# Two of the four score joins of a chunked recurrence moved from VectorE's predicated copies to plain ScalarE copies

## The chip, the core and the metric

The kernel runs on one core of one Trainium2 chip. Its metric is the device time of one launch in microseconds. Engines are named as in the profile: TensorE (PE, with PEld for its weight loads), VectorE (DVE), ScalarE (ACT), GpSimd (POOL), SyncE (SP).

## What is computed

The program is a model of two blocks, the first of two layers and the second of one. The change concerns one half of the first layer's mixer, a gated linear recurrence over 768 tokens (256 of context, 512 of the sequence) in 4 heads of 128 columns, once forwards and once backwards. Cut to what matters:

```python
def gla_chunked(q, k, v, log_f, s0):
    def step(state, inp):
        qc, kc, vc, gc = inp
        b = jnp.cumsum(gc, axis=2)
        diff = b[:, :, :, None, :] - b[:, :, None, :, :]
        decay = jnp.where(prefix_mask, jnp.exp(jnp.minimum(diff, 0.0)), 0.0)
        scores = jnp.einsum('bhtk,bhsk,bhtsk->bhts', qc, kc, decay)
        out = (jnp.einsum('bhtk,bhkv->bhtv', qc * jnp.exp(b), state)
               + jnp.einsum('bhts,bhsv->bhtv', scores, vc))
        b_last = b[:, :, -1:, :]
        new_state = (jnp.exp(b_last[:, :, 0, :])[..., None] * state
                     + jnp.einsum('bhsk,bhsv->bhkv', kc * jnp.exp(b_last - b), vc))
        return new_state, out
```

The scores have a decay that depends on the query, the key and the column, so they are no single matrix product. The kernel splits the lower triangle of a chunk into blocks, each with a reference token of its own, for which the decay falls into a factor of the query and a factor of the key.

## The kernel before, in words

**The stretch.** `recurrence_and_mix` interleaves four programs on each engine: `flow` (L456 matmuls: 8 tiles of a projection with 1024 x 128 weights split in a high and a low part, three matmuls each), `flow_g` (4 more such tiles), `gl`, an object of the class `Recurrence`, and `cm` (`ChunkMix`, a small token mixer, its matmuls L1511 to L1536). Each program yields at slots; `even` gives each slot a due time, `merged` sorts all slots by due time, and `weave` writes the instructions of each engine in that order. So each engine has one order written out by hand, and an instruction that waits holds up all that stand behind it on its engine, whichever program they belong to. The due times of `gl` are 8 us a slot before the first step and 14.3 us after.

**The recurrence.** Chunks are of 128 tokens; there are 6 of them and two directions, so 12 steps n = 0 to 11, directions alternating. A slot has eight turns, and `turns` gives for each engine what it does in which turn and how many steps ahead. In slot s, for step n = s unless said:

- VectorE: turn 0 `merge` (L1278 four times, L1281), turn 1 `decayed_base` of the next step (L1245, L1246), turn 2 `decayed` of the next step (L1256 eight times, L1258, L1259; the products of queries and keys with their decays), turn 3 `keys` three steps ahead (L1198), turn 4 `both` and `update` (L1289; L1299, the state, four instructions), turns 5 to 7 the log sums of later steps (L1228, L1233, L1217, L1218, L1207).
- ScalarE: turn 0 `grow_base` of the next step (L1319 to L1321), turn 1 `grow` of the next step (L1327 and L1328, the exponentials, the last 128 x 2560), turn 4 `take` (L1339) and `log` (L1311), turn 6 `keys_back` of the next step (L1333, which copies the turned keys from PSUM).
- TensorE: turn 2 `read_out` (L1358, L1359), turn 3 `gain` (L1366), turn 5 `turn_keys` (L1375, four transposes; it waits for the update L1299) and the scores of joins 0 and 1 of the next step (L1386), turn 6 the scores of joins 2 and 3 (L1386), turn 7 the base scores (L1406).

Between these, ScalarE evicts the projections' accumulators with Gelu (L1451) or Silu (L1584), which need another table (ACT_TABLE_LOAD; L52 loads the table of Ln and Exp back), and makes w_hi, the high part of a coming weight tile (L337). GpSimd makes w_lo from it (L378).

**The joins.** `JOINED` is (128, 64, 32, 16), the sizes of the blocks that are joined from halves; inside blocks of `BASE` = 8 tokens the base scores stand. For each join the scores lie in half a PSUM bank (`ps_s[0]` holds joins 0 and 1, `ps_s[1]` joins 2 and 3; 64 late queries for each of the 4 heads, so 256 columns), for all 128 keys on the partitions. Only those of keys in the early half of the same block are wanted. `merge` writes them into S (an SBUF tile of 128 x 512) with a predicated copy under a mask, four in turn, each waiting for the one before it (the counter `merged`), and then the base scores (L1281). `read_out` multiplies S with the values. `scored` counts the three groups of scores of a step.

Of the kernel before, what the change touches and what calls it, by code (L numbers as in the profile page):

```python
# [7 lines left out]
ACT = mybir.ActivationFunctionType  # L8
# [8 lines left out]
CHUNK = 128  # L17
# [750 lines left out]
A_HEADS = 4  # L768
# [334 lines left out]
class Recurrence:  # L1103
# [3 lines left out]

    def __init__(self, K, c, q, v, z, masks, masks_in, work, taken):  # L1110
        nc = self.nc = K.nc
        self.K, self.q, self.v, self.z, self.masks_in = K, q, v, z, masks_in
        H = A_HEADS
        self.NL = NL = len(JOINED)
        self.W = W = H * CHUNK
        self.steps, self.first = TOK // CHUNK, CTX // CHUNK
        self.n = 2 * self.steps
        LATE = CHUNK // 2
        self.masks = masks
        U32 = mybir.dt.uint32  # L1120
        self.mask = [[masks[:, d, l * LATE:(l + 1) * LATE].bitcast(U32) for l in range(NL)]
                     + [masks[:, d, NL * LATE:NL * LATE + CHUNK].bitcast(U32)] for d in range(2)]
        self.rel = [taken(f"rel{d}", NL + 3, work) for d in range(2)]
        self.k, self.S, self.state = ([taken(f"{n}{d}", 1, work)[:, 0, :] for d in range(2)]
                                      for n in ("k", "S", "state"))
        self.kt = taken("kt", 1, work)[:, 0, :]
        self.eb_end = [c.enter_context(nc.sbuf_tensor(f"gl_eb_end{d}", [P, H], F32)) for d in range(2)]
        bank = [c.enter_context(nc.psum_tensor(f"gl_bank{m}", [P, 512], F32)) for m in range(4)]
        self.ps_s, self.ps_u, self.ps_o = bank[0:2], bank[2], bank[3]
        (self.loaded, self.zeroed, self.k_done, self.logged, self.summed, self.related, self.grown, self.ends,  # L1130
         self.mixed, self.scored, self.merged, self.k_turned, self.kt_done, self.o_done, self.o_taken, self.u_done,
         self.updated) = K.signals("gl", "loaded zeroed k_done logged summed related grown ends mixed scored merged "
                                   "k_turned kt_done o_done o_taken u_done updated")

    SLOTS = range(-3, 12)

# [49 lines left out]
    def dve(self, dve):  # L1186
# [74 lines left out]
        def merge(n):  # L1261
            d = n % 2
            S = self.S[d]
            LATE = CHUNK // 2
            if n >= 2:
                dve.wait_ge(self.o_done, n - 1)
            for l, size in enumerate(JOINED):
                if l % 2 == 0:
                    dve.wait_ge(self.scored, 3 * n + l // 2 + 1)
                if l:  # L1270
                    dve.wait_ge(self.merged, 5 * n + l)
                nb, h = CHUNK // size, size // 2
                late, _ = self.late(d, size)
                out = self.heads(S).rearrange("p h (n e) -> p h n e", e=size)[:, :, :, late]
                mask = self.mask[d][l].rearrange("p (n e) -> p n e", e=h).unsqueeze(1).to_broadcast([P, H, nb, h])
                at = (l % 2) * H * LATE
                got = self.ps_s[l // 2][:, at:at + H * LATE].rearrange("p (h n e) -> p h n e", h=H, e=h)
                nc.vector.copy_predicated(out, mask, got).then_inc(self.merged, 1)  # L1278
            dve.wait_ge(self.scored, 3 * n + 3)
            dve.wait_ge(self.merged, 5 * n + NL)  # L1280
            nc.vector.copy_predicated(self.heads(S), self.mask[d][NL].unsqueeze(1).to_broadcast([P, H, CHUNK]),  # L1281
                                      self.heads(self.ps_o[:, :])).then_inc(self.merged, 1)

# [22 lines left out]
    def act(self, act):  # L1306
        nc, NL = self.nc, self.NL

        def log(n):
            act.wait_ge(self.k_done, n + 1)  # L1310
            nc.scalar.activation(self.of_z(n), self.of_z(n), ACT.Ln).then_inc(self.logged, 1)  # L1311

        def grow_base(n):
            d = n % 2
            act.wait_ge(self.related, 2 * n + 1)
            if n >= 2:
                act.wait_ge(self.updated, n - 1)
            end = 0 if d else CHUNK - 1
            nc.scalar.activation(self.eb_end[d][:, :], self.of_z(n)[:, :, end], ACT.Exp)  # L1319
            nc.scalar.activation(self.rel[d][:, NL + 1, :], self.rel[d][:, NL, :], ACT.Exp, scale=-1.0)  # L1320
            nc.scalar.activation(self.rel[d][:, NL + 2, :], self.rel[d][:, NL + 2, :], ACT.Exp).then_inc(self.grown, 1)  # L1321

        def grow(n):
            d = n % 2
            act.wait_ge(self.related, 2 * n + 2)
            act.wait_ge(self.grown, 2 * n + 1)
            nc.scalar.activation(self.of_z(n), self.of_z(n), ACT.Exp)  # L1327
            nc.scalar.activation(self.rel[d][:, 0:NL + 1, :], self.rel[d][:, 0:NL + 1, :],  # L1328
                                 ACT.Exp).then_inc(self.grown, 1)

        def keys_back(n):
            act.wait_ge(self.k_turned, n + 1)
            nc.scalar.activation(self.kt, self.ps_u[:, :], ACT.Copy).then_inc(self.kt_done, 1)  # L1333

        def take(n):
            if self.earlier(n) is not None:
                return
            act.wait_ge(self.o_done, n + 1)
            nc.scalar.activation(self.of_z(n), self.heads(self.ps_o[:, :]), ACT.Copy).then_inc(self.o_taken, 1)  # L1339
        yield from self.turns({0: [(1, grow_base)], 1: [(1, grow)], 4: [(0, take), (3, log)],  # L1340
                               6: [(1, keys_back)]})

    def pe(self, pe):
        nc, H, NL = self.nc, A_HEADS, self.NL
# [4 lines left out]

        def read_out(n):  # L1350
            d = n % 2
            pe.wait_ge(self.merged, 5 * n + 5)
            pe.wait_ge(self.mixed, n + 1)
            if n >= 2:
                pe.wait_ge(self.updated, n - 1)
            for h in range(H):
                c = self.col(h)
                nc.tensor.matmul(self.ps_o[:, c], self.state[d][:, c], self.of_z(n)[:, h, :], start=True, stop=False)  # L1358
                last = nc.tensor.matmul(self.ps_o[:, c], value(n, h), self.S[d][:, c], start=False, stop=True)  # L1359
            last.then_inc(self.o_done, 1)  # L1360
# [29 lines left out]
        def scores(n, half):  # L1390
            if n == 0 and half == 0:
                self.K.keep_busy(self.ps_s[0][:, 0:P], 18)
            pe.wait_ge(self.mixed, n + 1)
            if n:
                pe.wait_ge(self.merged, 5 * (n - 1) + 2 * half + 2)
            for l in (2 * half, 2 * half + 1):
                last = score(n, l)
            last.then_inc(self.scored, 1)
# [2539 lines left out]
```

## Time and profile before

| | us |
|---|---|
| median of 3 runs | 2659.57 |
| lowest and highest run | 2657.66 and 2663.55 |
| profiled execution, its own time | 2655.66 |
| profiled execution, its span | 2653.9 |

In the rows further down, a line of the timeline gives start and duration in us, engine, line, operation, output<-input, and in brackets the idle time of the engine before it with what ended it. A line of the waits says who waited for whom: us in total, times, longest. A line of the groups has count, busy us, mean ns of one, then the idle time before them. A line of the stages gives the stretch, its length, busy us of each engine with its count, the granted clock of TensorE (1.00 is full) and DMA. Matmuls are pipelined, so the duration of a group of them is longer than their number times their spacing.

### The profile page before, as it was taken

To read this page: it belongs to the slowest core of one execution; us is meant where nothing else is said; L and a number is where in the kernel's file an instruction comes from. 1 tells how busy PE (TensorE), PEld (TensorE's weight loads), DVE (VectorE), ACT (ScalarE), POOL (GpSimd) and SP (SyncE) were. 2 spreads that over 40 slices of the span, in tenths; PEclk is the share of its full clock that TensorE was granted. 3 is DMA by queue.
4 is the path that set the end of the run, shared out by engine and by line. 5 is a ranking of instruction groups with operands and counts; after the bars stand their busy time and mean duration, and the time that the engine had idled before them with its cause. 6 is when DMAs were issued, how large, how long until landed. Compare 5 with 4: busy or idle time off the path is not lost. (4 is left out here: it accounts for less than half of the span.)

```text
span 2653.9 us, 36467 instructions
## 1 busy us (share of the span) xinstructions
PE 2516.1 (95%) x14777; PEld 2127.7 (80%) x14777; DVE 1677.8 (63%) x2692; ACT 989.1 (37%) x1362; POOL 183.3 (7%) x185
## 2 busy tenths in 40 slices
PE   8999897999999999989999999999989988989997
PEld 3888786888888888866679989977778886867786
DVE  5887797467667776534446756737977775354744
ACT  4235555332212222345434323325532224345532
POOL 0111013000000000012000000001510000000000
PEclk9999999999999999999999999999999999999999
DMA  7650012223353333221023443322210001212232
GB/s 266 197 156 24 18 33 70 90 88 92 103 154 112 104 105 102 75 71 48 1 72 125 134 148 126 114 85 72 87 59 17 9 17 40 95 60 68 80 104 79
DMA packets 62682, 232.26 MB, mean 88 GB/s; under 512 B 6962, under 2 KB 9650, under 8 KB 61875
## 3 DMA queue, kind: packets, MB, share of 16 engines
q1 hardware_dynamic: 47538, 175.40, 20.2%
q0 software_dynamic: 14976, 54.53, 6.5%
q8 instruction: 117, 1.92, 0.3%
q14 instruction: 51, 0.41, 0.1%
HBM read 227.02 MB, written 2.10 MB: 86 GB/s over the span
## 5 line engine op out<-in xcount | busy, mean ns | idle before, releaser
L393 DVE TENSOR_TENSOR w_lo<-w_raw,w_hi 128x1024 fp32r<-128x1024 f32 (+2 forms) x253 | 323.0, 1277 | 322.2 <-ACT w_hi L337 318.1
L337 ACT ACTIVATE w_hi<-w_raw 128x1024 fp32r<-128x1024 f32 (+4 forms) x284 | 298.1, 1050 | 254.6 <-PE late_acc L474 93.4
L474 PE MATMUL mid_acc<-mid_h_hi,w_hi 128*128 128x258 f32 x832 | 279.7, 336 | 1.5 <-DVE mid_od_fq L642 1.0
L474 PE MATMUL mid_acc<-mid_h_hi,w_lo 128*128 128x258 f32 x832 | 279.3, 336 | 0.0
L474 PE MATMUL mid_acc<-mid_h_lo,w_hi 128*128 128x258 f32 x832 | 277.4, 333 | 0.0
L474 PE MATMUL late_acc<-late_h_hi,w_hi 128*128 128x258 f32 x704 | 199.4, 283 | 0.0
L474 PE MATMUL late_acc<-late_h_hi,w_lo 128*128 128x258 f32 x704 | 198.7, 282 | 0.0
L474 PE MATMUL late_acc<-late_h_lo,w_hi 128*128 128x258 f32 x704 | 197.9, 281 | 0.0
L474 PEld LDWEIGHTS mid_acc<-mid_h_hi,w_hi 128*128 128x128 f32 x832 | 157.5, 189 | 19.3 <-issue 2.4
L474 PEld LDWEIGHTS mid_acc<-mid_h_lo,w_hi 128*128 128x128 f32 x832 | 157.7, 190 | 18.5 <-issue 1.2
L474 PEld LDWEIGHTS mid_acc<-mid_h_hi,w_lo 128*128 128x128 f32 x832 | 157.0, 189 | 16.0
L474 PEld LDWEIGHTS late_acc<-late_h_lo,w_hi 128*128 128x128 f32 x704 | 133.8, 190 | 0.5 <-issue 0.5
L474 PEld LDWEIGHTS late_acc<-late_h_hi,w_hi 128*128 128x128 f32 x704 | 133.3, 189 | 0.5 <-issue 0.5
L474 PEld LDWEIGHTS late_acc<-late_h_hi,w_lo 128*128 128x128 f32 x704 | 132.9, 189 | 0.0
L474 PE MATMUL mid_acc<-mid_y_hi,w_lo 128*128 128x256 f32 (+1 forms) x384 | 128.8, 336 | 0.0
L474 PE MATMUL mid_acc<-mid_y_hi,w_hi 128*128 128x256 f32 (+1 forms) x384 | 128.0, 333 | 0.7 <-PEq L1744 0.7
L474 PE MATMUL mid_acc<-mid_y_lo,w_hi 128*128 128x256 f32 (+1 forms) x384 | 128.6, 335 | 0.0
L131 DVE CUSTOM_DVE_ANT_0 mid_scratch<-mid_side_raw,mid_rows 128x1024 f32<-128x1024 f32 x96 | 117.4, 1223 | 1.9 <-DVE mod L136 0.3
L2991 ACT ACTIVATE dr_low<-dr_bank 128x512 f32<-128x512 f32 x48 | 28.7, 597 | 173.0 <-PE dr_bank L3122 173.0
L474 PE MATMUL dq_acc<-s_h_hi,w_hi 128*128 128x512 f32 x200 | 85.8, 429 | 5.6 <-DVE s_h_lo L2577 4.2
L474 PE MATMUL qvz_acc<-ev_h_hi,w_hi 128*128 128x256 f32 (+1 forms) x256 | 87.2, 341 | 0.0
L474 PE MATMUL qvz_acc<-ev_h_lo,w_hi 128*128 128x256 f32 (+1 forms) x256 | 86.9, 340 | 0.0
(531 smaller groups left out, 6187.4 us busy)
## 6 DMA issues: line engine op xcount, KB each, us to landing
w_raw<-in_up SPq DMA_DIRECT2D x88, 512.0 KB, 3.6
mid_side_raw<-in_ada_t POOLq DMA_DIRECT2D x48, 512.0 KB, 3.9
w_raw<-in_down SPq DMA_DIRECT2D x32, 704.0 KB, 4.1
qvz_side_raw<-in_ada_t POOLq DMA_DIRECT2D x32, 512.0 KB, 4.0
w_raw<-in_dn_qkv SPq DMA_DIRECT2D x25, 512.0 KB, 3.2
late_side_raw<-in_ada_t POOLq DMA_DIRECT2D x24, 512.0 KB, 3.9
w_raw<-in_da SPq DMA_DIRECT2D x18, 512.0 KB, 3.3
w_raw<-in_ev_qvz SPq DMA_DIRECT2D x16, 512.0 KB, 4.2
```

The costliest lines, as they stand in the source:

```text
L131: nc.vector.tensor_tensor_reduce(out=self.scratch, in0=self.raw[:, j, :], in1=self.rows[:, m, :], scale=1.0, scalar=0.0, op0=ALU.mult, op1 ...
L337: nc.scalar.activation(K.whi[:, g % 2, 0:width], K.raw[:, g % 2, 0:width], ACT.Copy).then_inc(K.hi_done, 1)
L393: nc.vector.tensor_tensor(K.wlo[:, g % 2, 0:width], K.raw[:, g % 2, 0:width], K.whi[:, g % 2, 0:width].bitcast(F32), ALU.subtract).then_in ...
L474: last = nc.tensor.matmul(self.acc[i % len(self.acc)][:, at:at + width], left[:, j, cols], right[k][:, moving:moving + width], start=(k == ...
L2991: nc.scalar.activation(XL[G][:, :], bank[G][0][:, :], ACT.Copy).then_inc(A[G].empty, 1)
```

## The change

Joins 0 and 1 (sizes 128 and 64) have halves of 64 and 32 keys, which are whole ranges of partitions. For them ScalarE now writes the wanted scores to S with plain copies: one of 64 partitions x 256 (join 0) and two of 32 partitions x 128 (join 1), in the new `place`, in turn 6 of the slot before, behind `keys_back` of the same step. `place` waits for `scored` of joins 0 and 1 and, from step 2 on, for the read-out of the step that used the same S. It signals `placed`. On VectorE `merge` waits for `placed` and for the scores of joins 2 and 3, and does joins 2 and 3 and the base: three predicated copies instead of five. On TensorE the scores of joins 0 and 1 wait for `placed` of the step before, those of joins 2 and 3 and the read-out for the new counts of `merged`.

```diff
+    PLACED = 2
+    MERGES = len(JOINED) - PLACED + 1
...
@@ merge, on VectorE
-            if n >= 2:
-                dve.wait_ge(self.o_done, n - 1)
-            for l, size in enumerate(JOINED):
-                if l % 2 == 0:
-                    dve.wait_ge(self.scored, 3 * n + l // 2 + 1)
-                if l:
-                    dve.wait_ge(self.merged, 5 * n + l)
+            dve.wait_ge(self.placed, n + 1)
+            dve.wait_ge(self.scored, 3 * n + 2)
+            for l in range(self.PLACED, NL):
+                size = JOINED[l]
+                if l > self.PLACED:
+                    dve.wait_ge(self.merged, self.MERGES * n + l - self.PLACED)
...
-            dve.wait_ge(self.merged, 5 * n + NL)
+            dve.wait_ge(self.merged, self.MERGES * n + NL - self.PLACED)
...
@@ on ScalarE
+        def place(n):
+            d = n % 2
+            if n == 0:
+                act.wait_ge(self.zeroed, 1)
+            if n >= 2:
+                act.wait_ge(self.o_done, n - 1)
+            act.wait_ge(self.scored, 3 * n + 1)
+            for l in range(self.PLACED):
+                size = JOINED[l]
+                nb, h = CHUNK // size, size // 2
+                late, early = self.late(d, size)
+                out = self.heads(self.S[d]).rearrange("p h (n e) -> p h n e", e=size)
+                at = l * A_HEADS * (CHUNK // 2)
+                got = self.ps_s[0][:, at:at + A_HEADS * (CHUNK // 2)].rearrange("p (h n e) -> p h n e", h=A_HEADS, e=h)
+                for m in range(nb):
+                    keys = slice(m * size + early.start, m * size + early.stop)
+                    last = nc.scalar.activation(out[keys, :, m, late], got[keys, :, m, :], ACT.Copy)
+            last.then_inc(self.placed, 1)
...
-                               6: [(1, keys_back)]})
+                               6: [(1, keys_back), (1, place)]})
...
@@ on TensorE
-            pe.wait_ge(self.merged, 5 * n + 5)
+            pe.wait_ge(self.merged, self.MERGES * (n + 1))
...
-                pe.wait_ge(self.merged, 5 * (n - 1) + 2 * half + 2)
+                if half == 0:
+                    pe.wait_ge(self.placed, n)
+                else:
+                    pe.wait_ge(self.merged, self.MERGES * (n - 1) + NL - self.PLACED)
```

## Rows read from the trace of the kernel before

**Rows 1.** The page, busy us, share of the span and instructions of each engine:

```profile
PE 2516.1 (95%) x14777; PEld 2127.7 (80%) x14777; DVE 1677.8 (63%) x2692; ACT 989.1 (37%) x1362; POOL 183.3 (7%) x185
```

**Rows 2.** The stages (stretch; busy us of PE, PEld, DVE, ACT, POOL; clock; DMA):

```profile
205.00:437.50 232.50, 219.73 (x1535) 198.45 (x1533) 177.50 (x412) 125.99 (x169) 27.27 (x12) 0.98 0.08 24
```

**Rows 3.** The waits from 205 to 445 us:

```profile
ACT x L1333 <- PE gl_bank L1375: 21.9, 7, 7.2
...
DVE x L1281 <- PE gl_bank L1406: 8.5, 8, 2.1
...
DVE ev_rest L1256 <- ACT ev_rest L1328: 7.3, 7, 2.7
...
PE gl_bank L1375 <- DVE ev_rest L1299: 4.3, 4, 2.3
```

**Rows 4.** The timeline of step n = 6 on TensorE, ScalarE and VectorE:

```profile
341.35 0.60 PE L1375 MATMUL gl_bank<-ident,ev_rest 128*128 128x128 f32 x4
341.79 1.90 PE L1386 MATMUL gl_bank<-ev_rest 128*128 128x64 f32 x16
...
341.99 0.60 ACT L1333 ACTIVATE x<-gl_bank 128x512 f32<-128x512 f32 x1 [1.60 <-PE gl_bank L1375]
342.61 1.28 ACT L1451 ACT_TABLE_LOAD   x1
343.90 0.88 ACT L1451 ACTIVATE x<-uv_acc 128x512 f32<-128x512 f32 x2
...
348.92 2.33 ACT L1328 ACTIVATE ev_rest<-ev_rest 128x2560 f32<-128x2560 f32 x1
...
351.28 0.43 DVE L1256 TENSOR_TENSOR ev_rest<-ev_q,ev_rest 128x256 f32<-128x256 f32 x1
...
356.11 1.12 DVE L1299 SCALAR_TENSOR_TENSOR ev_rest<-ev_rest,gl_eb_end,gl_bank 128x128 f32<-128x128 f32 x4 [0.39 <-PE gl_bank L1366]
...
357.29 0.66 PE L1375 MATMUL gl_bank<-ident,ev_rest 128*128 128x128 f32 x4 [0.50 <-DVE ev_rest L1299]
```

**Rows 5.** The groups by line and shape, 205 to 445 us:

```profile
L1278 DVE COPY_PREDICATED x<-rstd,gl_bank 128x256 f32<-128x256 uint32 x48 | 21.2, 441 | 18.8 <-PE gl_bank L1386 17.2
...
L1451 ACT ACTIVATE x<-uv_acc 128x512 f32<-128x512 f32 x7 | 4.2, 597 | 0.1
...
L1451 ACT ACTIVATE x<-uv_acc 128x256 f32<-128x256 f32 x7 | 2.7, 379 | 0.0
```

**Rows 6.** The timeline of VectorE, joins of n = 6, base copy of n = 7:

```profile
347.17 1.97 DVE L1278 COPY_PREDICATED x<-rstd,gl_bank 128x256 f32<-128x256 uint32 x4
...
367.36 0.75 DVE L1281 COPY_PREDICATED x<-rstd,gl_bank 128x512 f32<-128x512 uint32 x1 [1.02 <-PE gl_bank L1406]
```

**Rows 7.** The timeline of the three engines, single rows of other steps:

```profile
268.22 0.58 ACT L1481 ACTIVATE x<-cm_ps,eps 128x384 f32<-128x384 f32 x1 [5.03 <-PE cm_ps L1511]
...
325.32 0.66 PE L1375 MATMUL gl_bank<-ident,ev_rest 128*128 128x128 f32 x4 [2.32 <-DVE ev_rest L1299]
...
360.54 1.06 ACT L337 ACTIVATE w_hi<-w_raw 128x1024 fp32r<-128x1024 f32 x1 [1.96 <-PE uv_acc L456]
...
386.82 0.43 DVE L1256 TENSOR_TENSOR ev_rest<-ev_q,ev_rest 128x256 f32<-128x256 f32 x1 [0.48 <-ACT ev_rest L1328]
...
400.36 2.33 ACT L1328 ACTIVATE ev_rest<-ev_rest 128x2560 f32<-128x2560 f32 x1
...
403.51 0.41 DVE L1256 TENSOR_TENSOR ev_rest<-ev_q,ev_rest 128x256 f32<-128x256 f32 x1
...
414.85 0.38 ACT L1584 ACTIVATE x<-uv_acc 128x256 f32<-128x256 f32 x1 [1.35 <-PE uv_acc L456]
```

**Rows 8.** A stall in TensorE's timeline, and the stages after two stalls:

```profile
363.93 0.47 PE L456 MATMUL uv_acc<-ev_h_hi,w_hi 128*128 128x512 f32 x1 [1.75 <-ACT x L1451]
...
365.50:368.50 3.00, 3.00 (x13) 2.71 (x12) 1.95 (x4) 2.91 (x4) 0.00 (x0) 0.50 0.42 164
...
325.50:329.00 3.50, 3.50 (x27) 3.24 (x27) 3.50 (x10) 2.95 (x5) 0.00 (x0) 1.00 0.00 0
```

More of the change, by code:

```diff
@@ L1131, in __init__ @@
          self.mixed, self.scored, self.merged, self.k_turned, self.kt_done, self.o_done, self.o_taken, self.u_done,
-         self.updated) = K.signals("gl", "loaded zeroed k_done logged summed related grown ends mixed scored merged "
-                                   "k_turned kt_done o_done o_taken u_done updated")
+         self.updated, self.placed) = K.signals("gl", "loaded zeroed k_done logged summed related grown ends mixed scored merged "
+                                   "k_turned kt_done o_done o_taken u_done updated placed")
     SLOTS = range(-3, 12)
```

## The prediction

> **What bounds the kernel now.** The page first: TensorE is busy for 95% of the span [rows 1]. The first layer's recurrence is only the stretch from 205 to 437.5 us; there the stages row shows TensorE busy for 219.7 of 232.5 us, VectorE for 177.5 and ScalarE for 126.0 [rows 2]. So in this stretch time is lost or won only where TensorE stands still, and next I read which wait ends last there. In the waits of the stretch TensorE waits for VectorE's state update (L1299) before it turns the keys (L1375), for 4.3 us in all; VectorE in its turn waits for ScalarE's large exponential (L1328) before the scaling products (L1256), 7.3 us in 7 waits; and ScalarE waits for TensorE's turned keys (L1375) before it copies them (L1333), 21.9 us [rows 3]. These three waits close a ring: turned keys, copy, other ScalarE work, exponentials, products, update, next turned keys.
>
> The timeline of one step (n = 6) shows the ring go round [rows 4]. TensorE turns the keys at 341.35 and then does the scores of the first two joins, 341.79 to 343.69. ScalarE copies the keys at 341.99 and goes straight on to a table load at 342.61, the two Gelu evictions, w_hi, and the exponentials, whose last ends at 351.25. VectorE starts the products at 351.28, the moment the last exponential is there, is through them and a later step's keys at 355.72, waits 0.39 us for TensorE and updates from 356.11 to 357.23. TensorE, which has stood for 0.50 us, turns the next keys at 357.29. Everything in this ring from 342.61 to 351.25 is ScalarE in program order, with no wait in it.
>
> **What goes.** Two predicated copies of 128x256 on VectorE per step: 24 of them at 441 ns [rows 5], 10.6 us of VectorE; with their wait for each other they stand 0.49 us apart (four take 1.97 us [rows 6]), so 0.98 us per step. Is any of it on the path? No. What follows the joins is the base copy (L1281), and that needs the base scores, which TensorE does last: at n = 7 the base copy waits 1.02 us for them [rows 6], and 8.5 us in 8 waits over the stretch [rows 3]. At n = 6 the four joins end at 349.14 and the copy follows in line, but behind it come only L1245 and L1246 before VectorE needs L1328, which ends at 351.25 [rows 4]. So the freed 0.98 us ends in waits that are there already: I credit 0. The bound on the gain: five steps (n = 4, 5, 6, 8, 9) have four joins in one run, 4.9 us if VectorE set the pace in all of them.
>
> **What is added.** Three plain copies from PSUM per step on ScalarE: 64 partitions x 256, and 32 x 128 twice, 36 in all. The trace has no such copy. ScalarE's time goes by elements of a partition: 597 ns for 512, 379 for 256 [rows 5], so 0.85 ns each and by extension 270 ns for 128. An ACTIVATE behind another starts about 0.10 us before that ends (597 + 379 = 976 ns, but the two evictions take 0.88 us together [rows 4]). So three in a row take 0.28 + 0.17 + 0.27 = 0.72 us, say 0.71. Bounds: 0.55 us if narrow copies are cheaper, 0.92 us if nothing overlaps. The page "ScalarE: Activation LUTs" of the Trainium skill, section "Rules for kernel authors", tells authors to leave such simple work to VectorE and prices each ACTIVATE at about 0.3 us plus 0.83 ns an element; by that three would take about 1.33 us, and the sum below would be some 3 us larger. The 597 ns row lies below what that gives for 512 elements (0.72 us), so I keep to the rows.
>
> **The added wait** is the larger part. The copies stand right behind the keys' copy and wait for the scores of the first two joins. At n = 6 these end at 343.69, the keys' copy at 342.59: ScalarE stands 1.14 us (with 0.04 us for the signal, as between the end of L1375 at 341.95 and 341.99), copies for 0.71 us, and starts the table load at 344.46 instead of 342.61: **1.85 us late**. Queued behind it on ScalarE are the evictions, w_hi (GpSimd's w_lo and the next weight load wait for that; these have a tile of 16 us to spare) and the exponentials, for which VectorE waits, for which TensorE waits. No DMA is moved.
>
> Step by step, what reaches TensorE's next turn of the keys:
> - n = 0 to 3: another activation holds the keys' copy up until the scores are done, and 0.7 us goes into ScalarE's next waits, such as 5.03 us before 268.22 [rows 7]. At n = 0 alone such a wait comes only after the exponentials. 0.
> - n = 4: scores long done, the copies advance ScalarE by 0.60 us (what follows overlaps the last), and the products waited on L1328 as at n = 8; TensorE's 2.32 us stall at 325.32 grows: 0.6 [rows 7].
> - n = 5 and 6: 1.85 less VectorE's 0.39 us of slack before the update; n = 5 runs as n = 6 does, with 0.05 us more between update and turn: 1.4 and 1.5 [rows 4].
> - n = 7: ScalarE waits 1.96 us for TensorE before w_hi at 360.54 anyway, and the copies fit before it: 0 [rows 7].
> - n = 8: the products at 386.82 wait on L1328 and VectorE has no slack after them: 1.85 [rows 7].
> - n = 9: L1328 would end at 404.54 instead of 402.69; VectorE began the products at 403.51, when itself ready: 1.05 [rows 7].
> - n = 10: the wait of 1.35 us before the second eviction at 414.85 absorbs most: 0.4 [rows 7].
> - n = 11: the same wait, longer: 0.
>
> Sum: 0.6 + 1.4 + 1.5 + 1.85 + 1.05 + 0.4 = **6.8 us** longer. TensorE is already in its order of work, so nothing fills these stalls.
>
> **The clock.** After TensorE's 1.75 us stall before 363.93, a step with a 0.50 us stall before it, the granted clock falls to the lower level (1.2 GHz); it is 0.50 from 365.5 to 368.5 [rows 8]. After the stall of 2.32 us before 325.32 it stays full [rows 8]. Three microseconds at half clock lose 1.5 us of matmuls. The change makes five stalls of 1 us or more at L1375: 2.32 + 0.6 = 2.9 after n = 4, then 1.4, 0.5 + 1.5 = 2.0, and 1.85 and over 1.05 after n = 8 and 9. One of these two brought a fall; part of the loss lies beside ScalarE's chain. I take two falls worth 1 us each, between 0 and 5 x 1.5 = 7.5: +2.
>
> The sum is made against the profiled execution, 2655.66 us with a span of 2653.9; that gives 2664.5. The median of the runs is 3.9 us higher at 2659.57, and the same 8.8 us on it gives 2668.4: **2668.0 us**.
>
> **Rivals.**
> 1. VectorE sets the pace (faster). If ScalarE's delay were taken up by slack, each step with joins in one run would save 0.98 us; TensorE's waits for the update (4.3 us) cap it there: 2659.6 - 4.3 = 2655.3. For it: VectorE is the engine that TensorE waits for at L1375 [rows 3], and all five steps have their joins in one run. Against it: the products start on L1328's end at n = 6 and 8 [rows 4, 7], and VectorE waits for it 7 times in all [rows 3]. It decides if ScalarE's chain is under 0.1 us late at the products. Chance 0.07.
> 2. Nothing to be measured. The delay is half absorbed: only n = 5, 6 and 8 carry it, less VectorE's 0.98 where it helps, and no fall of the clock, (1.4 + 1.5 + 1.85) less 0.98 = 3.8 us: 2663.4. A measurement of this kernel can tell about 0.2%, 5.3 us, from no change, and my sum without the clock is only 1.5 us above that. Chance 0.2.
> 3. The ring with more clock falls: each new stall brings one, inside the scores for which ScalarE now waits, so that the loss goes into the ring in full: 6.8 + 7.5 = 14.3 us, 2673.9. Chance 0.15, part of slower.
> 4. The forecast, 0.58.
>
> **Numbers.** Slower 0.73 (forecast and rival 3), same 0.20, faster 0.07. The range 2661 to 2675 holds most of rival 2 at its lower end and rival 3 at its upper; it leaves out rival 1 and combinations with dearer copies.
>
> **What would show it.** In the profile after: three ACTIVATEs beside L1333 per step, the first waiting for L1386 about 1.1 us at n = 5, 6, 8, 9, 10; L1278 with 24 instead of 48; L1256's wait for L1328 up from 7.3 to about 15 us; TensorE's wait for L1299 at L1375 up from 4.3 to 10 or more; the stretch 205 to 437.5 longer by 7 to 9 us, nothing changed before 315 us. It is wrong if the step from one L1375 to the next stays at 16.0 us around n = 5 and 6, or if L1256 no longer waits for ScalarE.

## The result, and the profile after

The changed kernel takes 2675.19 us (median of 4 runs, 2674.52 to 2678.01) against 2658.61 us before: a ratio of 1.0057 with an interval of 1.0044 to 1.0069. It is **slower**: by 0.57%, 15 us, by the ratio, and by 16.6 us between the medians. Run once more, beside other runs of the kernel before, it gave 1.0063 (1.0048 to 1.0078). The line numbers of the kernel after have moved: the turned keys are L1396, the joins' scores L1407, the keys' copy L1335, the large exponential L1330, the products L1259, the update L1301, joins 2 and 3 L1280, the new copies L1353.

The profiled execution took 2675.26 us with a span of 2673.5. From the first turning of the keys to the last update it is 240.28 us long, against 226.31 before. The page's first part, and the stages of these two stretches, after and then before:

```profile
PE 2535.0 (95%) x14777; PEld 2141.2 (80%) x14777; DVE 1667.4 (62%) x2668; ACT 999.5 (37%) x1398; POOL 183.3 (7%) x185
```

```profile
211.58:451.86 240.28, 225.63 (x1510) 204.11 (x1508) 161.12 (x371) 135.10 (x203) 26.13 (x11) 0.94 0.06 21
```

```profile
210.10:436.41 226.31, 214.63 (x1510) 193.92 (x1508) 171.53 (x396) 124.89 (x167) 26.38 (x11) 0.98 0.07 22
```

So 14.0 us of the difference lie in the stretch. VectorE has 10.4 us less to do there, as foreseen, and ScalarE 10.2 us more, against 8.5 by the forecast's 0.71 us a step. TensorE, with the same number of matmuls, is busy 11.0 us longer, and its granted clock is 0.94 instead of 0.98: its work has not grown, it runs slower. Its idle time has grown by 3.0 us. (The rest of the difference between these two executions, 5.6 us, lies outside, 1.5 us ahead of the stretch and 4.2 us behind it, where the programs are the same; runs of the kernel before spread from 2656.5 to 2668.2 us.)

The waits of the kernel after, 205 to 465 us (the rows that answer to [rows 3], with the new ones):

```profile
ACT x L1335 <- PE gl_bank L1396: 20.7, 7, 7.3
...
DVE x L1283 <- PE gl_bank L1430: 16.2, 10, 3.8
...
ACT x L1353 <- PE gl_bank L1407: 11.8, 7, 2.8
DVE ev_rest L1259 <- ACT ev_rest L1330: 10.3, 9, 3.4
...
PE gl_bank L1396 <- DVE ev_rest L1301: 8.6, 5, 2.8
```

The third line is the wait that the change adds, 11.8 us of ScalarE. (VectorE's joins now wait for the copies too, 12.6 us in 3 times, all at steps 0 to 4.) TensorE's wait for the update has doubled, from 4.3 to 8.6 us. And VectorE's base copy (L1283), which waited 8.5 us for the base scores, now waits 16.2: that is where VectorE's freed time went, for the most part.

Step n = 6 in the timelines of ScalarE, VectorE and TensorE, to be laid beside [rows 4]:

```profile
345.68 0.66 PE L1396 MATMUL gl_bank<-ident,ev_rest 128*128 128x128 f32 x4 [0.29 <-DVE ev_rest L1301]
346.18 1.90 PE L1407 MATMUL gl_bank<-ev_rest 128*128 128x64 f32 x16
...
346.38 0.60 ACT L1335 ACTIVATE x<-gl_bank 128x512 f32<-128x512 f32 x1 [1.11 <-PE gl_bank L1396]
348.17 0.81 ACT L1353 ACTIVATE x<-gl_bank 64x256 f32<-64x256 f32 x3 [1.20 <-PE gl_bank L1407]
349.00 1.28 ACT L1475 ACT_TABLE_LOAD   x1
...
355.31 2.33 ACT L1330 ACTIVATE ev_rest<-ev_rest 128x2560 f32<-128x2560 f32 x1
...
357.67 0.42 DVE L1259 TENSOR_TENSOR ev_rest<-ev_q,ev_rest 128x256 f32<-128x256 f32 x1 [0.49 <-ACT ev_rest L1330]
...
363.20 0.81 PE L1396 MATMUL gl_bank<-ident,ev_rest 128*128 128x128 f32 x4 [2.07 <-DVE ev_rest L1301]
```

ScalarE stands 1.20 us for the scores, copies for 0.81 us, and loads the table at 349.00, 3.32 us after the keys were turned; before it was 341.35 to 342.61, 1.26 us. From this turning to the next it is 17.52 us instead of 15.94, with a stall of TensorE of 2.07 us instead of 0.50. The step is as the prediction drew it (ScalarE is 2.06 us late, 1.85 was forecast).

What comes behind that stall is not. The stages of the kernel after around three of the stalls (behind steps 4, 6 and 8):

```profile
328.00:334.00 6.00, 6.00 (x36) 5.44 (x35) 5.00 (x15) 4.00 (x8) 0.00 (x0) 0.72 0.00 0
363.00:376.00 13.00, 12.63 (x54) 11.89 (x55) 6.19 (x17) 8.57 (x14) 2.35 (x1) 0.52 0.14 42
404.00:415.00 11.00, 11.00 (x50) 10.48 (x51) 5.88 (x16) 7.64 (x13) 0.31 (x1) 0.53 0.01 2
```

TensorE is busy nearly without a gap in all three, but the granted clock is 0.72, 0.52 and 0.53: it has fallen to the lower level (1.2 GHz). The first fall covers 3 to 4 us, the second some 13 us (single microseconds show 1.00 again from 378 on), the third some 10 us (1.00 again from 415 on). Before it fell in this part once, for 3 us [rows 8].

### The profile page after: what moved, and what is told of

It reads as the page before. It is cut to its first block and busy times, and to the rows that moved or that the text cites. A ratio compares the mean times of both kernels' runs of the same rounds, so it can differ in the third digit from the quotient of the medians.

```text
span 2673.5 us, 36480 instructions
## 1 busy us (share of the span) xinstructions
PE 2535.0 (95%) x14777; PEld 2141.2 (80%) x14777; DVE 1667.4 (62%) x2668; ACT 999.5 (37%) x1398; POOL 183.3 (7%) x185
## 3 DMA queue, kind: packets, MB, share of 16 engines
q8 instruction: 117, 1.92, 0.3%
```

## The measure for the experiments

The time of a run moves by several microseconds with what the clock does elsewhere. The stretch is a better measure: the intervals between two turnings of the keys (starts of the TensorE rows of four transposes in the timeline), steps 0 to 1, 1 to 2 and so on. In us:

```
                    0-1   1-2   2-3   3-4   4-5   5-6   6-7   7-8   8-9  9-10 10-11 | all
before            26.02 22.93 24.48 22.54 19.25 16.03 15.94 19.51 16.15 16.21 16.90 | 215.96
after             26.01 22.92 24.46 22.57 20.09 18.05 17.52 22.61 18.07 20.10 17.53 | 229.93
h_after_again     26.03 22.94 24.50 22.55 20.08 20.80 17.47 22.64 18.07 20.11 17.52 | 232.71
e1_place_late     26.02 24.03 25.65 25.63 20.07 17.62 16.27 18.54 17.04 17.69 22.40 | 230.96
e2_wait_only      25.99 22.98 24.55 22.56 19.25 17.61 15.94 20.83 16.15 16.96 16.90 | 219.72
e3_copies_only    26.03 22.94 24.46 22.57 20.20 17.63 16.27 17.91 16.87 16.97 20.82 | 222.67
e4_fill           26.02 22.93 24.44 22.55 20.08 17.63 17.51 19.57 18.05 17.70 17.57 | 224.05
f1_before_fill    26.02 22.92 24.49 22.55 19.25 16.04 15.92 19.52 16.15 16.20 16.90 | 215.96
f2_copies_fill    26.01 22.94 24.43 22.56 20.21 16.49 16.27 19.53 16.87 16.96 16.90 | 219.17
f3_wait_fill      26.02 22.93 24.48 22.55 19.94 16.88 16.82 17.90 17.42 16.96 16.90 | 218.80
f4_place_late5    26.02 22.93 24.46 22.56 20.07 16.60 16.34 18.54 17.03 17.70 17.57 | 219.82
g1_before_fill7   26.02 22.93 24.40 22.56 19.25 16.04 15.93 17.92 16.15 16.20 16.90 | 214.30
```

Steps 0 to 3 are equal to 0.1 us in all kernels but e1_place_late. The changed kernel's 13.97 us all arise from step 4 on: 0.84, 2.02, 1.58, 3.10, 1.92, 3.89 and 0.63. The prediction had 0.6, 1.4, 1.5, 0, 1.85, 1.05 and 0.4.

## Experiments

Theory: a ring of waits through ScalarE, lengthened by the wait for the scores and by the copies, and, on top, the clock that falls after the stalls. Rivals: the copies as such; and VectorE's freed time, which counts once nothing holds ScalarE up.

### Is it the clock? TensorE filled in its stalls (e4_fill)

```diff
+    FILL = {5: 12, 6: 6, 7: 8, 9: 8, 10: 7, 11: 5}
...
         def turn_keys(n):
+            if n in self.FILL:
+                pe.wait_ge(self.placed, n)
+                self.K.keep_busy(self.ps_s[0][:, 0:P], self.FILL[n])
             if n:
                 pe.wait_ge(self.updated, n)
```

> The changed kernel with TensorE kept busy by matmuls into an unread score bank (12, 6, 8, 8, 7 and 5 of them at steps 5, 6, 7, 9, 10 and 11) ahead of its wait for the state update, where it otherwise stands still. If 7 of the 14 us are the granted clock that falls after the new stalls: the clock stays at 0.98 or more in the stretch, the distance from first to last turning of the keys falls from 229.9 to 223 us, and the time is 6 to 9 us above before. If the clock's fall costs nothing that is not hidden beside ScalarE's chain: no change against the changed kernel, 14 to 17 us above before.

Measured: 2669.2 us (10 runs), ratio 1.0027 (1.0015 to 1.0039); stretch 224.05 us. The filling matmuls (each has two rows in the profile, so 12 are 24), the stall that is left, and the stages of this kernel behind steps 4, 6 and 8:

```profile
323.30 2.84 PE L57 MATMUL gl_bank<-ident 128*128 128x128 f32 x24
326.30 0.66 PE L1400 MATMUL gl_bank<-ident,ev_rest 128*128 128x128 f32 x4 [0.16 <-DVE ev_rest L1302]
```

```profile
326.00:337.00 11.00, 10.84 (x72) 9.68 (x71) 9.46 (x20) 8.64 (x14) 2.42 (x1) 1.00 0.00 1
363.00:376.00 13.00, 11.05 (x62) 9.66 (x62) 10.16 (x21) 9.53 (x13) 2.35 (x1) 0.87 0.14 41
403.00:415.00 12.00, 12.00 (x83) 10.98 (x83) 7.77 (x20) 8.00 (x9) 2.38 (x1) 1.00 0.13 46
```

Matmuls whose result nobody reads make the changed kernel 5.9 us faster in the stretch, because the clock stays full behind the stalls that they fill. One fall is left (0.87 in the second stage), behind another stall, of 1.95 us before 368.28 at step 7, where the kernel before has one of 1.75 us and a fall as well [rows 8]. The intervals that shrink are the three with a fall: 5-6 by 0.42, 7-8 by 3.04 and 9-10 by 2.40 us. What is left above before, 8.1 us, is the ring: 0.83, 1.60, 1.57, 0.06, 1.90, 1.49, 0.67. (So of the 11.0 us that TensorE was busy longer, 5.9 us lengthen the stretch; the other 5.1 passed in time in which it would otherwise have stood, since its idle time grew by 3.0 us and not by 8.1.)

### Is that the same each time? The changed kernel once more (h_after_again)

> The changed kernel once more, unaltered, to see how much of its time is the same in every execution. By the filled kernel 8.1 us of the 14 us in the stretch are fixed (waits and copies) and 5.9 us are falls of the granted clock after steps 5, 7 and 9, which may move or vary: intervals between the turns of the keys from step 4 on of at least 20.1, 17.6, 17.5, 19.5 (17.9 without a fall), 18.0, 17.7 and 17.5, distance 222 to 231 us, time 9 to 17 us above before.

Measured: 2678.29 us (4 runs), ratio 1.0063 (1.0048 to 1.0078); stretch 232.71 us. The falls after steps 7 and 9 are there again, to 0.03 us the same; the one after step 5 is longer (20.80 instead of 18.05 us; 0.61 from 327 to 340 us), which puts the stretch 1.7 us above what was expected. So the clock takes 5.9 us in one execution and 8.7 in the other.

### The same fill on the kernel before (f1_before_fill)

```diff
+    FILL = {5: 10, 7: 2, 10: 3, 11: 3}
+            if n in self.FILL:
+                pe.wait_ge(self.merged, 5 * (n - 1) + 2)
+                self.K.keep_busy(self.ps_s[0][:, 0:P], self.FILL[n])
```

> The kernel before, with TensorE kept busy (10, 2, 3 and 3 matmuls into an unread score bank) where it stands ahead of the update at steps 5, 7, 10 and 11. The matmuls take no longer than the stalls, so they cost nothing; if a stall of 2.3 us now and then pulls the clock down in the kernel before too (the wait-only kernel showed 17.6 us instead of 16.0 between the turns of steps 5 and 6, with nothing on ScalarE delayed), the distance from first to last turning is 215 to 216.5 us and the time 0 to 3 us below before. If the clock has nothing to do with it, no change, and the fill can only cost: 0 to 2 us above.

Measured: 2662.34 us, ratio 1.0004 (0.9994 to 1.0014), not to be told from before; stretch 215.96 us, equal to before. The fill costs nothing and, as in the profiled execution before the clock had fallen only at step 7, gains nothing. This is the base line for the next two.

### The wait and the copies apart (e2_wait_only, e3_copies_only, then f2_copies_fill, f3_wait_fill)

```diff
         def keys_back(n):
             act.wait_ge(self.k_turned, n + 1)
             nc.scalar.activation(self.kt, self.ps_u[:, :], ACT.Copy).then_inc(self.kt_done, 1)
+            act.wait_ge(self.scored, 3 * n + 1)
```

> The kernel before with one thing added: ScalarE waits for the scores of the first two joins behind the keys' copy; nothing is copied, VectorE does all joins. Ring theory: 1.14 us late at steps 5, 6, 8, 9, 10, of which 0.7, 0.75, 1.1, 0.35 and 0 reach TensorE: 2.9 us, plus 0 to 4 us for the clock: 3 to 7 us slower than before. Rival (the copies are what costs): no change within 1 us. If the wait carries nearly all, with the clock: 10 us or more.

Measured: 2665.2 us, ratio 1.0010 (0.9999 to 1.0020), not to be told from before; stretch 219.72 us. The sum fits the expectation, the steps do not: 5-6 is 1.58 longer and 6-7 not at all. ScalarE's timeline says why:

```profile
326.62 0.60 ACT L1333 ACTIVATE x<-gl_bank 128x512 f32<-128x512 f32 x1 [1.11 <-PE gl_bank L1376]
327.23 1.28 ACT L1452 ACT_TABLE_LOAD   x1
328.55 0.87 ACT L1452 ACTIVATE x<-uv_acc 128x512 f32<-128x512 f32 x2
```

The table load starts 0.01 us behind the keys' copy, as if no wait stood there; only the activation behind it is held, and by then the scores are done. So in these steps this run doesn't test the wait, and its longer 5-6 is the clock (0.84 from 325 to 336 us), after a 2.30 us stall that the kernel before has as well; the longer 7-8 goes with a clock of 0.81 from 360 to 378 us. Only at n = 9, where an activation and not a table load stands behind the keys' copy, was ScalarE held, for 1.14 us, and 9-10 is 0.75 longer. The run also shows that the fall after step 5 can strike a kernel with ScalarE on time.

Three copies without the wait, to an unread tile; the signal `kt_done` comes from the last of them:

```diff
+            for rows, cols in ((slice(0, 64), 256), (slice(64, 96), 128), (slice(96, 128), 128)):
+                last = nc.scalar.activation(self.spare[rows, 0:cols], self.ps_u[rows, 0:cols], ACT.Copy)
```

> The kernel before with three copies more on ScalarE behind the keys' copy, of the shapes of the change, from the bank of the turned keys to an unread tile, without the wait for the scores; VectorE does all joins. Ring theory: 0.6, 0.3, 0.3 and 0.7 us at steps 4, 5, 6 and 8 and nothing at 9 and 10: 1.9 us, plus up to 2 us for the clock: 2 to 4 us slower than before. Rival (the copies are what costs): 12 us or more.

Measured: 2666.36 us, ratio 1.0021 (1.0012 to 1.0031); stretch 222.67 us. It has a fall of the clock in 10-11, which is 3.9 us longer for it, and none in 7-8 (17.91 instead of 19.51), so I took both tests again with the fill. For the wait, a copy of one column (0.17 us) now follows it, so that the table load can't go ahead; VectorE's joins and TensorE's next scores wait for `spared`:

```diff
+            act.wait_ge(self.scored, 3 * n + 1)
+            nc.scalar.activation(self.spare[:, 0:1], self.ps_s[0][:, 0:1], ACT.Copy).then_inc(self.spared, 1)
```

The fills are sized to each kernel's stalls: {5: 12, 6: 2, 7: 3, 9: 3, 10: 6, 11: 4} matmuls in f2_copies_fill, {5: 11, 6: 4, 7: 6, 9: 6, 10: 5, 11: 4} in f3_wait_fill.

> Copies on ScalarE behind the keys' copy without a wait for the scores, as in the copies-only kernel, and TensorE kept busy in its stalls, so that the clock is out of the comparison. Ring theory: over the kernel before with the fill 0.9, 0.3, 0.3, 0, 0.7, 0.4 and 0 us from step 4 on, 2.6 in all: distance first to last turning about 218.5 us. Rival (copies are the main cost): 222 us and more.

> The kernel before with ScalarE made to wait for the scores of the first two joins by a copy of one column (0.2 us) behind the keys' copy, since a bare wait let the table load go ahead of it; TensorE kept busy in its stalls. ScalarE goes on 1.3 us late. Ring theory: 0.1, 0.9, 0.9, 0, 1.3, 0.5 and 0 us over before from step 4 on, 3.7 in all: distance about 219.5 us. If the wait is harmless: 216 us.

Measured, stretch above the filled kernel before: **copies 3.2 us** (0.96, 0.45, 0.35, 0.01, 0.72, 0.76, 0); **wait 4.5 us** (0.69, 0.84, 0.90, [7-8], 1.27, 0.76, 0), leaving out 7-8, where this kernel happens not to have the fall and is 1.6 us shorter. (Against g1_before_fill7 further down, which has no fall there either, 7-8 differs by 0.02 us and the whole by 4.5 us.) The 0.69 at 4-5 isn't the wait's: there the fill was too long. In this test all four joins wait for `spared`, the base copy and with it TensorE came late, and the fill of 11 matmuls ended only after the update:

```profile
323.94 1.11 DVE L1302 SCALAR_TENSOR_TENSOR ev_rest<-ev_rest,gl_eb_end,gl_bank 128x128 f32<-128x128 f32 x4
325.74 0.60 PE L1385 MATMUL gl_bank<-ident,ev_rest 128*128 128x128 f32 x4
```

The turn comes 0.69 us after the update's end instead of 0.06, so that the wait itself costs 0.06 at 4-5 (0.1 was expected) and **3.8 us** in all. ScalarE's timeline in the wait's kernel shows that in the steps of the ring the wait is tested now:

```profile
343.26 0.60 ACT L1336 ACTIVATE x<-gl_bank 128x512 f32<-128x512 f32 x1 [1.12 <-PE gl_bank L1385]
345.05 0.17 ACT L1340 ACTIVATE gl_spare<-gl_bank 128x1 f32<-128x1 f32 x1 [1.20 <-PE gl_bank L1396]
345.24 1.28 ACT L1463 ACT_TABLE_LOAD   x1
```

Together 7.0 us, against 8.1 us in the filled changed kernel. Both parts count, the wait somewhat more. The parts needn't add up: each alone is first taken up by slack (at 5-6 and 6-7 VectorE's 0.39 us, at 10-11 all of it), which the two together exceed; these three intervals make 1.3 us more together than one by one. The whole times of these two, 2664.25 us (ratio 1.0005, 0.9995 to 1.0016) and 2662.82 us (1.0005, the same interval), can't tell such sums from nothing.

The copies alone lengthen 9-10 by 0.76 us. The expectation had 0.4 there, and by the prediction's account, in which 0.82 us of slack stood before the products, a delay of 0.8 us would have cost nothing. Why the slack isn't there in this kernel, the timelines of VectorE and GpSimd tell. From f2_copies_fill:

```profile
404.59 2.90 DVE L1248 TENSOR_TENSOR ev_rest<-x,ev_rest 128x512 f32<-128x512 f32 x1
407.41 0.41 DVE L1258 TENSOR_TENSOR ev_rest<-ev_q,ev_rest 128x256 f32<-128x256 f32 x1
```

```profile
404.12 2.82 POOL L378 TENSOR_TENSOR w_lo<-w_raw,w_hi 128x1024 fp32r<-128x1024 f32 x1 [15.78 <-ACT w_hi L337]
```

A VectorE operation of 0.68 us elsewhere takes 2.90 us and ends 0.55 us after GpSimd's w_lo, as if it had begun when w_lo was through (406.94). The Trainium skill, "SBUF — State Buffer", section "SBUF: two separate sides", says that VectorE operations with two SBUF inputs and GpSimd hold one shared pair of ports in turn, each for its whole instruction; these rows agree. So at this step VectorE's start of the products hangs on w_lo, hence on w_hi, hence again on ScalarE. The same happens in the wait's kernel (2.90 us) and in e2_wait_only (2.88 us). It does not happen in the changed kernel: with two joins less, VectorE is through with this operation at 408.24 in e4_fill, just before w_lo begins at 408.39, and the products wait for the exponentials alone. So the 0.76 us in either test is not a price that the change pays at 9-10, and the split between wait and copies is not exact there.

### The copies elsewhere (e1_place_late, f4_place_late5)

```diff
-        yield from self.turns({0: [(1, grow_base)], 1: [(1, grow)], 4: [(0, take), (3, log)],
-                               6: [(1, keys_back), (1, place)]})
+        yield from self.turns({0: [(0, place), (1, grow_base)], 1: [(1, grow)], 4: [(0, take), (3, log)],
+                               6: [(1, keys_back)]})
```

> The three copies are issued one turn group later on ScalarE, ahead of the next step's exponentials of the ends (L1321), so that for steps 5, 6, 7 and 8 they stand behind the evictions and w_hi, when the scores have long been done; for steps 9 to 11 the order is that of the changed kernel. Ring theory (the wait for the scores holds ScalarE's chain, and stalls then pull the clock down): the wait of 1.1 us goes for 5, 6 and 8, only 0.7 us of copies stays there; the distance from the first to the last turning of the keys falls from 229.9 us to 219.3 (216.0 before, plus 0.6, 0.3, 0.3, 0.7, 1.05 and 0.4) with 0 to 4 us more for the clock: 3 to 8 us slower than before in all. Rival (any added ScalarE work costs this much, the wait is incidental): stays within 2 us of the changed kernel, 14 to 16 us slower than before. Rival (VectorE's freed time counts once the wait is gone): faster than before by up to 4 us.

Measured: 2673.38 us, ratio 1.0046 (1.0029 to 1.0063); stretch 230.96 us: a miss. The time is that of the rival in which any added work of ScalarE costs this much, but the steps don't bear it out. Where the wait goes, the intervals do shrink: 6-7 is 16.27 and 8-9 17.04. But two things take that back. In steps 1 to 3 the copies now stand ahead of an activation of the small mixer, which TensorE waits for in the end:

```profile
273.76 0.52 PE L1549 MATMUL cm_ps<-ident,x 128*128 128x128 f32 x3 [3.92 <-DVE x L1572]
```

(2.73 us before), so that 1-2, 2-3 and 3-4 are 1.1, 1.2 and 3.1 us longer. And the clock is 0.50 from 420 to 430 us, which makes 10-11 22.40. With the late place from step 5 on alone, and a fill of {5: 12, 6: 2, 7: 3, 9: 4, 10: 7, 11: 5}:

```diff
+    LATE_FROM = 5
+        def early(stage):
+            return lambda n: stage(n) if n < self.LATE_FROM else None
+        def late(stage):
+            return lambda n: stage(n) if n >= self.LATE_FROM else None
+        yield from self.turns({0: [(0, late(place)), (1, grow_base)], 1: [(1, grow)], 4: [(0, take), (3, log)],
+                               6: [(1, keys_back), (1, early(place))]})
```

> The changed kernel with the copies moved behind the evictions and w_hi from step 5 on only (steps 0 to 4 as in the change, so that the small mixer's activations are not delayed), and TensorE kept busy in its stalls. Ring theory: against the changed kernel with the fill (224.05 us) the waits of 1.1 us go at steps 5, 6 and 8: intervals 20.1, 16.4, 16.3, 19.5, 17.0, 17.7, 17.6, distance about 220.4 us, time 3 to 6 us above before. If VectorE's freed 0.98 us counts once the wait is gone: 216 us or less. If only the clock was at fault: no gain over 224 us.

Measured: 2663.6 us, ratio 1.0012 (1.0003 to 1.0022); stretch 219.82 us. The waits cost what was said: 4.2 us less than e4_fill, 1.0, 1.2 and 1.0 us of it at 5-6, 6-7 and 8-9, and 1.0 at 7-8, where no fall came this time (clock 1.00 from 360 to 378 us). VectorE's relief shows no gain yet: all intervals from 4 on but 7-8 are above those of before.

### Can the stall at step 7 be had back? (g1_before_fill7)

```diff
             last.then_inc(self.scored, 1)
+            if half == 1 and n == 7:
+                pe.wait_ge(self.o_taken, n)
+                self.K.keep_busy(self.ps_o[:, 0:P], 7)
```

> The filled kernel before, with 7 more matmuls behind the second half of step 7's scores, where TensorE stands 1.75 us for the last Gelu eviction ahead of the next projection. In the wait-only kernel with the fill the clock did not fall there and the interval from step 7 to 8 was 17.9 us instead of 19.5. So: that interval 17.9 us, distance first to last turning 214.4 us. If the fall is not the cause of the difference: 19.5 and 216.0.

The kernel also keeps the fills of f1_before_fill. Measured: 2659.85 us, ratio 0.9993 (0.9982 to 1.0003), not to be told from before; stretch 214.30 us, 7-8 17.92, as expected if the fall is the cause. Stages, with this fill and without it (f1_before_fill):

```profile
360.00:372.00 12.00, 11.87 (x81) 10.74 (x81) 11.63 (x23) 8.76 (x11) 2.56 (x1) 1.00 0.15 44
```

```profile
360.00:372.00 12.00, 10.25 (x55) 9.10 (x55) 10.67 (x22) 8.60 (x10) 2.55 (x1) 0.86 0.15 44
```

A stall of 1.75 us, filled, gives 1.6 us back that came after it.

### Taking ScalarE out of the ring (g2_before_reorder, g3_after_reorder)

From step 5 on TensorE does the first scores ahead of turning the keys, and ScalarE's keys' copy stands in the next turn, behind `grow_base`. `early` and `late` are those of f4_place_late5, with LATE_FROM = 5; of the fills only g1_before_fill7's at step 7 is kept. On the kernel before, TensorE's line and then ScalarE's:

```diff
-        yield from self.turns({2: [(0, read_out)], 3: [(0, gain)], 5: [(1, turn_keys), (1, lambda n: scores(n, 0))],
+        yield from self.turns({2: [(0, read_out)], 3: [(0, gain)],
+                               5: [(1, lambda n: turn_keys(n) if n < self.LATE_FROM else None), (1, lambda n: scores(n, 0)),
+                                   (1, lambda n: turn_keys(n) if n >= self.LATE_FROM else None)],
...
-        yield from self.turns({0: [(1, grow_base)], 1: [(1, grow)], 4: [(0, take), (3, log)],
-                               6: [(1, keys_back)]})
+        yield from self.turns({0: [(1, grow_base), (0, late(keys_back))], 1: [(1, grow)], 4: [(0, take), (3, log)],
+                               6: [(1, early(keys_back))]})
```

and on the kernel after, ScalarE's:

```diff
+        yield from self.turns({0: [(0, late(place)), (1, grow_base), (0, late(keys_back))], 1: [(1, grow)],
+                               4: [(0, take), (3, log)], 6: [(1, early(keys_back)), (1, early(place))]})
```

> The kernel before, from step 5 on with TensorE's scores of the first two joins ahead of the turning of the keys (they don't need the state, so they fill its wait for the update), and ScalarE's copy of the keys behind the exponentials of the ends, so that ScalarE no longer waits for TensorE inside the ring; 7 filling matmuls at step 7. Then VectorE's own work sets the pace, about 15.6 us a step instead of 16.0: distance 3 to 5 us below before. If the ring goes through ScalarE's other work anyway: within 1 us of before.

> The same two moves on the changed kernel, its copies too behind w_hi from step 5 on. VectorE has 0.98 us less to do in a step than in the reordered kernel before; if VectorE then sets the pace in five steps, this one is 1 to 3 us shorter than that, and 4 to 7 us shorter than before. If TensorE's own work (15.4 us a step) is the bound by then, the two are within 1 us of each other; if the copies on ScalarE still count, this one is the longer by 1 to 3 us.

From step 5 on the keys are turned behind the scores, so their distance can't be compared with that of the other kernels; from the first turning to the last update it is 226.31 us before, 224.65 in g1_before_fill7, **224.18** in g2 and **224.27** in g3. Times: 2660.25 us (0.9994, 0.9983 to 1.0004) and 2659.4 us (0.9991, 0.9981 to 1.0000). No measurement here tells them from before. Most of their 2 us is the filled stall of step 7. The forecast of 3 to 5 us for the one, and more for the other, was too much. The number of the third branch came, the two within 1 us; its reason, that TensorE is the bound by then, is not shown. Stages from 315 to 434 us, of g2 and then of g3,

```profile
315.00:434.00 119.00, 114.11 (x837) 106.11 (x836) 107.98 (x247) 69.71 (x88) 18.94 (x8) 1.00 0.08 28
```

```profile
315.00:434.00 119.00, 114.27 (x834) 105.99 (x833) 99.57 (x231) 77.77 (x113) 18.41 (x8) 1.00 0.09 28
```

VectorE is busy for 8.4 us less in g3 and ScalarE for 8.1 us more; TensorE is busy for 114 of 119 us in both, at full clock. But the same sum hides opposite steps. The turnings of the two kernels can be compared with each other: from 4-5 on g3 is longer by 0.84, -0.67, -1.01, 0.01, 0, 0.65 and 0.24 us. The two steps that are shorter are steps in which TensorE waits in g2, before the read-out, for VectorE's base copy. In g3 the first of these waits has shrunk and the second is gone (g2, then g3):

```profile
336.79 0.49 PE L1365 MATMUL gl_bank<-ev_z,ev_rest 128*128 128x128 f32 x2 [0.98 <-DVE x L1282]
...
354.21 0.49 PE L1365 MATMUL gl_bank<-ev_z,ev_rest 128*128 128x128 f32 x2 [1.01 <-DVE x L1282]
```

```profile
337.38 0.49 PE L1386 MATMUL gl_bank<-ev_z,ev_rest 128*128 128x128 f32 x2 [0.32 <-DVE x L1284]
```

So with ScalarE out of the ring VectorE's relief was worth 1.7 us in two steps, and the other steps took as much back: VectorE waits for the exponentials for 11.5 us from 300 to 440 us in g3, for 4.8 us in g2.

## Why the prediction was right or wrong

- **The sign, and the ring: right.** Slower was given 0.73. The wait of 1.14 us at n = 6 measured 1.20, the interval grew by 1.58 us (1.5 forecast), TensorE's stall from 0.50 to 2.07 (2.0 forecast). VectorE's part was credited with 0. In the change its freed time did end in the wait for the base scores; but at n = 9 it kept VectorE clear of w_lo, which held it in e2_wait_only, f2_copies_fill and f3_wait_fill, with all joins on VectorE, and with ScalarE out of the ring (g2, g3) it was worth 1.7 us in two steps. The 0 holds for the kernel as it was, not for one in which ScalarE keeps up.
- **The sum of the ring: a little low,** 6.8 forecast, 8.1 measured in e4_fill. The copies were sized 0.71 us; they take 0.80 on even steps and 0.94 on odd ones, since not all of them overlap, and neither does the activation behind them. (The dearer price that the prediction quotes from the Trainium skill, "ScalarE: Activation LUTs", section "Rules for kernel authors", stands there for an ACTIVATE whose bias is a pointer operand; these copies are given no bias, and came to 0.94 us at most, not 1.33.) At n = 4 that made 0.83 of 0.6, at n = 10 0.67 of 0.4. At n = 9 it made 1.49 of 1.05: the slack of 0.82 us was there as read, but ScalarE was 2.26 us late in e4_fill and not 1.85 (wait 1.20, copies 0.94, and 0.1 of lost overlap).
- **The term that failed: "I take two falls worth 1 us each".** The clock cost 5.9 us in the first profiled execution and 8.7 in the second. The rows for it were those of the kernel before, with one fall of 3 us; in the kernel after two of three falls last some 13 and 10 us. Why they last that long no run here shows. What they do is in the rows: with a slower TensorE ScalarE waits longer for the scores (2.77 us at n = 7 and 2.67 at n = 9, in e4_fill 1.20 at both), so that the loss goes into the ring; filled stalls give it back. Rival 3 had this mechanism and nearly this sum, 14.3 against 14.0, but the sum is luck in part: it took 6.8 for the ring and 7.5 for five falls, and 8.1 and 5.9 with three falls came, in the second execution 8.1 and 8.7. It should have been nearer to the forecast's middle.
- **The number:** 2668.0 forecast, 2675.19 measured, 0.2 us above the upper end of 2661 to 2675; by the ratio of 1.0057, on the 2659.57 us that the forecast was made on, it is 2674.7, just inside. A change of 8.4 us was forecast, 15 us by the ratio and 16.6 us between the medians came: the sign and the chain of causes are right, the size of the clock's part is not.
- **What would show it:** 24 L1280, three copies a step, nothing changed before 315 us: so. The stretch longer by 7 to 9 us: 14.0. TensorE's wait for the update 10 us or more: 8.6. The products' wait for the exponentials "about 15 us": 10.3; where the rest went was not followed up.

## What to carry to other kernels

An engine that is idle for two thirds of the time may still be in series with the bound: before work is moved to it, follow what stands behind the place where it goes in, and price the added wait before the added work. Where TensorE is near its full load, a stall of 2 us has to be priced with the clock that follows, which here cost 5.9 and 8.7 us beside 8.1 us of stalls; a few unread matmuls in a stall show in one run how much of a slowdown is of that kind. And relief for an engine is worth what its successor's wait says: VectorE's here ended in a wait for TensorE's base scores that was already in the profile. And when two kernels come out equal, compare them step by step: g2 and g3 are equal in sum and differ by up to 1.0 us in single steps. A fill, too, has to be checked in the trace: one that is a little too long looks like the effect that is being measured.

## What was not expected of the hardware

- The granted clock fell to the lower level after stalls of 1.5 to 2.8 us, but not after each. Behind step 4 in the kernel before, after 2.32 us, it stayed full; in e2_wait_only, after 2.30 us, it was 0.84 over 11 us. After the stall of 1.75 us at step 7 it fell in the kernel before and in f1_before_fill and stayed full in f3_wait_fill and f4_place_late5. After 1.49 us at 412.71 it was 0.57 for 7 us in e3_copies_only, and after 1.49 us at 413.42 it stayed full in e2_wait_only. Two executions of the changed kernel had the same falls at steps 7 and 9 to 0.03 us, and different ones at step 5 (18.05 and 20.80 us).
- A wait written between an activation and the Gelu activation that needs another table did not hold the table load: it began 0.01 us after the activation before it. The program doesn't name this load, so it may stand ahead of the wait in the instructions; the trace doesn't tell. An activation of one column behind the wait did hold it.
- Three small copies from PSUM of 64 x 256, 32 x 128 and 32 x 128 take 0.79 to 0.81 us together on even steps and 0.94 on odd ones; singly 0.375 and 0.264 us. It isn't the direction as such: f2_copies_fill copies the same partitions in every step and takes 0.93 in all. The single rows show what differs. At n = 6 the second copy (partitions 0 to 31, behind 0 to 63) begins at 348.45, 0.10 us before the first ends, and the third (64 to 95) at 348.71, 0.01 us after the second. At n = 7 (64 to 127, then 32 to 63, then 96 to 127), and in f2_copies_fill (0 to 63, 64 to 95, 96 to 127), none of them overlaps. In the rows read, an activation overlapped the one ahead only where its partitions were among those of the one ahead; whether that is the rule was not tested.
